# Late modulation with an output per partition: row sums on VectorE and one transposition per chunk

## What is computed

```python
def _modulation(cond, w_mod, b_mod):
    m = jax.nn.silu(cond) @ w_mod + b_mod          # cond [1024], w_mod [1024, 3072]
    return jnp.split(m, 3, axis=-1)
...
h = x * (1.0 + sc) + sh                            # before layer l's input projection
...
x_new = _layer_norm(DEEPNORM_ALPHA * x + (1.0 + g) * out, ln_g[l], ln_b[l])
```

## Time and profile before

| | us |
|---|---|
| median of 3 runs | 1850.63 (1850.36 to 1851.28) |
| the profiled execution, its own time | 1850.39 |
| its span in the profile | 1848.6 |
| PE busy | 1802.8 (98%) |
| DVE busy | 1291.5 (70%) |
| ACT busy | 928.0 (50%) |

### The profile page before, as it was taken

How to read it: one execution, slowest core, us unless ns; L and a number is a source line. 1 busy time by engine, 2 the same in 40 slices (tenths; PEclk the granted TensorE clock), 3 DMA queues, 4 the chain that set the end, 5 groups by cost and what they waited for, 6 DMA issues and landing times. The chain is left out here.

```text
span 1848.6 us, 30835 instructions
## 1 busy us (share of the span) xinstructions
PE 1802.8 (98%) x10621; PEld 1554.1 (84%) x10621; DVE 1291.5 (70%) x2061; ACT 928.0 (50%) x1680; POOL 269.4 (15%) x219
## 2 busy tenths in 40 slices
PE   7999999999999999989999999999999999999998
PEld 3888888888888888878878889888888888898886
DVE  6677777778687877765868485675848484757658
ACT  2555555555555555560046555464736464554500
POOL 3100000000000000255431010101000010102951
PEclk9999999999999999999999999999999999999999
DMA  9512121312122222225420010101010100101343
GB/s 348 135 47 83 47 82 47 84 38 79 54 74 60 74 60 62 73 94 187 159 80 24 12 45 11 45 0 45 11 45 11 34 23 11 45 11 45 99 143 125
DMA packets 82111, 127.28 MB, mean 69 GB/s; under 512 B 49760, under 2 KB 49920, under 8 KB 81936
## 3 DMA queue, kind: packets, MB, share of 16 engines
q1 hardware_dynamic: 76048, 108.54, 18.7%
q0 software_dynamic: 2384, 8.39, 1.6%
q10 hardware_dynamic: 3632, 9.73, 1.3%
HBM read 108.90 MB, written 20.09 MB: 70 GB/s over the span
## 5 line engine op out<-in xcount | busy, mean ns | idle before, releaser
L548 PE MATMUL acc<-h_hi,w_hi 128*128 128x512 f32 (+1 forms) x1408 | 524.9, 373 | 3.1 <-DVE h_lo L473 1.6
L548 PE MATMUL acc<-h_hi,w_lo 128*128 128x512 f32 (+1 forms) x1408 | 508.7, 361 | 0.0
L548 PE MATMUL acc<-h_lo,w_hi 128*128 128x512 f32 (+1 forms) x1408 | 507.9, 361 | 0.0
L548 PEld LDWEIGHTS acc<-h_hi,w_lo 128*128 128x128 f32 x1408 | 265.3, 188 | 41.5
L548 PEld LDWEIGHTS acc<-h_hi,w_hi 128*128 128x128 f32 x1408 | 265.8, 189 | 40.3 <-DVE h_lo L473 4.7
L548 PEld LDWEIGHTS acc<-h_lo,w_hi 128*128 128x128 f32 x1408 | 266.3, 189 | 33.9
L1676 DVE TENSOR_REDUCE stats<-acc 128x1 f32<-128x1280 f32 x128 | 189.7, 1487 | 43.3 <-PE acc L1775 42.7
L1586 ACT ACTIVATE far_prob<-acc,stats 128x1280 f32<-128x1280 f32 x128 | 170.2, 1330 | 28.3 <-DVE stats L1676 26.5
L1593 ACT ACTIVATE far_pt<-acc 128x512 f32<-128x512 f32 (+1 forms) x192 | 101.1, 527 | 162.0 <-PE acc L1784 158.6
L1775 PE MATMUL acc<-k_dup,q_stack 128*128 128x512 f32 (+1 forms) x768 | 176.7, 367 | 1.8 <-ACT far_prob L1586 0.4
L1797 PE MATMUL acc<-far_pt,far_v 128*128 128x128 f32 x1280 | 172.7, 275 | 0.0
(11 more groups left out here) (208 smaller groups left out, 2906.8 us busy)
## 6 DMA issues: line engine op xcount, KB each, us to landing
w_raw<-in_w_in SPq DMA_DIRECT2D x64, 512.0 KB, 3.3
near_late_slots<-in_w_mod SPq DMA_DIRECT2D x64, 256.0 KB, 2.7
w_raw<-in_w_out SPq DMA_DIRECT2D x16, 512.0 KB, 3.2
w_raw<-y_t POOLq DMA_DIRECT2D x14, 448.0 KB, 5.0
y_t<-y SPq DMA_DIRECT2D x7, 640.0 KB, 3.1
modulation_rows<-in_w_scale SPq DMA_DIRECT2D x8, 512.0 KB, 6.9
modulation_rows<-in_w_mod SPq DMA_DIRECT2D x8, 512.0 KB, 6.7
out_rows<-in_x SPq DMA_DIRECT2D x8, 512.0 KB, 4.5
```

What stands on the lines that cost most here:

```text
L548: mm = nc.tensor.matmul(m.bank(self.bank_of(j, c), w), wt[:, b % 2, k, :], ht[:, k, t0:t0 + w], start=(k == 0 and i == 0), stop=(k == KT - ...
```

## The change

The weights of the late modulation are given transposed (`w_late`, 4096 x 1024): a tile is now 128 outputs, one per partition, by 512 inputs. A chunk's 512 outputs are four blocks of 128 (t = 0 to 3), each in two halves of the inputs; tile u is half u // 4, block u % 4. `sum(u)` is a `tensor_tensor_reduce` per vector: the tile times the condition laid along the row, summed along it, 128 x 512, with the sum of the first half as the start value of the second. The result is a column. After eight tiles there are 8 columns (two vectors, four blocks), and PE turns them once (`turn`), [128, 8] to [8, 128].

For this the condition has to stand in each partition as a row. At the start PE turns it, ACT copies it and SP stores it to HBM (`cond_rows`). In the chunks `load_coef` spreads half of it (512 values of both vectors) over 128 partitions: a copy of 512 KB, twice a chunk, into one buffer. The copy of the second half waits until `sum(3)` is done, `sum(4)` waits until it has landed.

The sums move too. `dve_part` now has 0, 1, (2, 3), (4, 5), (6), where it had 0, 1, 2, 3, 4; only `sum(7)` is left for the steps (step 7, in the last chunk step 3). The tile 7 is loaded with 5 and 6. `reduce_last` is gone. The row is stored by two copies in place of one.

```diff
     def load(self, sp, c, u):
         if u >= 2:
-            sp.wait_ge(self.summed, CREDIT + c * 2 * KT + 2 * (u - 1))
+            sp.wait_ge(self.summed, CREDIT + c * 2 * KT + 2 * (KT if u == KT else u - 1))
...
+    def load_coef(self, sp, c, half):
+
+        sp.wait_ge(self.summed, CREDIT + c * 2 * KT + KT * half)
+        first = self.cond_rows[0, half % 2 * 512:half % 2 * 512 + 1]
+        src = bass.AP(first.tensor, first.offset, [[0, P], [D, 2], [1, 512]])
+        sp.dma_start(self.coef, src).then_inc(self.coef_loaded, 16)
 
     def sum(self, v, c, u):
+
+        half, t = u // 4, u % 4
         v.wait_ge(self.loaded[u % 2], CREDIT + c * 8 * KT + 16 * (u // 2 + 1))
+        if t == 0:
+            v.wait_ge(self.coef_loaded, CREDIT + c * 32 + 16 * (half + 1))
         if u == 0:
-            v.wait_ge(self.reduced, CREDIT + c * 1)
+            v.wait_ge(self.turned, CREDIT + c * 1)
+        v.wait_ge(self.summed, CREDIT + c * 2 * KT + 2 * u)
+        x = self.slots[u % 2]
         for cnd in range(2):
...
-                ins = self.nc.vector.scalar_tensor_tensor(self.acc[cnd], x, coef, self.acc[cnd], ALU.mult, ALU.add)
-            ins.then_inc(self.summed, 1)
...
+            self.nc.vector.tensor_tensor_reduce(out=unused, in0=x, in1=self.coef[:, cnd, :], scale=0.5,
+                                                scalar=self.sums[:, 0, col:col + 1] if half else 0.0, op0=ALU.mult, op1=ALU.add,
+                                                accum_out=self.sums[:, half, col:col + 1]).then_inc(self.summed, 1)
...
+    def turn(self, pe, c, bank):
 
         pe.wait_ge(self.summed, CREDIT + c * 2 * KT + 2 * KT)
...
+        self.nc.tensor.transpose(self.m.psum[0:8, bank, 0:P], self.sums[:, 1, :], self.m.ident[:, :]).then_inc(self.turned, 1)
...
@@ dve_part
-        for j in range(6, self.cum[2]):
+        for j, sums in zip(range(6, self.cum[2]), ((2, 3), (4, 5), (6,))):
             self.split_x_lo(v, c, j)
-            late.sum(v, c, j - 4)
+            for u in sums:
+                late.sum(v, c, u)
...
@@ sync, chunk
-                    for u in (3, 4, 5, 6):
+                    for u in (3, 4):
+                        late.load(sp, c, u)
+                    late.load_coef(sp, c, 1)
+                    for u in (5, 6, 7):
                         late.load(sp, c, u)
...
@@ sync, start
                 modulation.load_weights(sp)
+                modulation.store_cond(sp)
                 load_first(sp)
...
                 if g == 1:
+                    sp.wait_ge(modulation.cond_stored, 16)
                     p[0].load(sp, 0, 1)
...
@@ vector, steps
-                        if step == 3 and last:
-                            late.sum(v, c, 5)
-                        if NU - 3 <= step < NU and not last:
-                            late.sum(v, c, step - NU + 3 + 5)
+                        if step == (3 if last else NU - 3):
+                            late.sum(v, c, KT - 1)
...
@@ tensor, step 10
-                            if last:
-                                late.reduce_last(pe, c, 1)
-                            else:
-                                late.reduce(pe, c, 7)
+                            late.turn(pe, c, 1 if last else 7)
```

More of the change, by code:

```diff
@@ L237, in activate @@
         act.wait_ge(self.small_in, 48)
-        self.nc.scalar.activation(self.m.cond_act[:, :, :], self.m.cond[:, :, :], ACT.Tanh, scale=0.5).then_inc(self.tanh_done, 1)
+        self.nc.scalar.activation(self.m.cond_act[:, :, :], self.m.cond[:, :, :], ACT.Tanh, scale=0.5).then_inc(self.act, 1)
     def exp_lambda(self, act):
         act.wait_ge(self.dve, 2)
-        self.nc.scalar.activation(self.sums[:, 2:4], self.sums[:, 0:2], ACT.Exp).then_inc(self.lam_exp, 1)
+        self.nc.scalar.activation(self.sums[:, 2:4], self.sums[:, 0:2], ACT.Exp).then_inc(self.act, 1)
     def take_rows(self, act):
@@ L368, with __init__ @@
     AHEAD = 2
-    def __init__(self, nc, m, near, stack, w_mod, mod_rows):
-        self.nc, self.m, self.w_mod, self.mod_rows = nc, m, w_mod, mod_rows
+    def __init__(self, nc, m, near, stack, w_late, cond_rows, mod_rows):
+        self.nc, self.m, self.w_late, self.cond_rows, self.mod_rows = nc, m, w_late, cond_rows, mod_rows
         sem = lambda n: stack.enter_context(nc.semaphore("x_" + n))
         self.slots = [near.late_slots[:, i, :] for i in range(2)]
-        self.acc = [near.late_acc[:, i, :] for i in range(2)]
-        self.row = near.late_row
+        self.coef, self.row, self.sums = near.late_coef, near.late_row, near.late_sums
+        self.unused = [near.prob[:, 2 + i, 0:512] for i in range(2)]
@@ L400, in sum @@
-            ins.then_inc(self.summed, 1)
-    def reduce(self, pe, c, bank):
-        pe.wait_ge(self.summed, CREDIT + c * 2 * KT + 2 * KT)
[L405 to L417, removed]
-            mm = self.nc.tensor.matmul(self.m.psum[0:2, bank, :], self.m.pick[:, cnd, :], self.acc[cnd],
-                                       start=False, stop=(cnd == 1))
-        mm.then_inc(self.reduced, 1)
+            col = cnd * 4 + t
@@ L422, in take_row @@
     def take_row(self, act, c, bank):
-        act.wait_ge(self.row_stored, CREDIT + c * 16)
-        act.wait_ge(self.reduced, CREDIT + c * 1 + 1)
-        self.nc.scalar.activation(self.row, self.m.psum[0:2, bank, :], ACT.Copy, scale=0.5).then_inc(self.row_ready, 1)
+        act.wait_ge(self.row_stored, CREDIT + c * 32)
+        act.wait_ge(self.turned, CREDIT + c * 1 + 1)
+        self.nc.scalar.activation(self.row, self.m.psum[0:8, bank, 0:P], ACT.Copy).then_inc(self.row_ready, 1)
     def store_row(self, sp, c):
@@ L428, in store_row @@
         sp.wait_ge(self.row_ready, CREDIT + c * 1 + 1)
-        sp.dma_start(self.mod_rows[:, bass.ds(c * 512 + ROW_PAD, 512)], self.row).then_inc(self.row_stored, 16)
+        for cnd in range(2):
+            sp.dma_start(self.mod_rows[cnd, bass.ds(c * 4 + ROW_PAD // P, 4), :], self.row[4 * cnd:4 * cnd + 4, :]).then_inc(self.row_stored, 16)
 TOKEN_TILES = [range(0, 4), range(4, 8), range(8, 10)]
@@ L961, in of_result, with neighbourhood @@
         return t.rearrange("p (b r n) -> p b r n", b=2, r=2) if self.local else t.rearrange("p (b n) -> p b n", b=2)
-def neighbourhood(nc, m, near, stack, p, modulation, tokens, x_in, load_first, all_counters, out_w, after, biases, w_mod, mod_rows, y_out):
+def neighbourhood(nc, m, near, stack, p, modulation, tokens, x_in, load_first, all_counters, out_w, after, biases, w_late, cond_rows, mod_rows, y_out):
     l = 0
@@ L979, in neighbourhood @@
     factors_ready, spread, gate_scaled = sem("factors_ready"), sem("spread"), sem("gate_scaled")
-    late = LateModulation(nc, m, near, stack, w_mod, mod_rows)
+    late = LateModulation(nc, m, near, stack, w_late, cond_rows, mod_rows)
     counters += late.counters
@@ L1086, in chunk @@
                             out_w.load(sp, p, k)
-                            if k == 3:
-                                late.load(sp, c, 7)
                     else:
@@ L1098, in chunk @@
                     if not last:
-                        for u in (7, KT, KT + 1):
+                        for u in (KT, KT + 1):
                             late.load(sp, c, u)
+                        late.load_coef(sp, c, 2)
                     late.store_row(sp, c)
@@ L1119, in _ @@
                     late.load(sp, 0, u)
+                late.load_coef(sp, 0, 0)
                 each_chunk(sp, chunk)
-                sp.wait_ge(late.row_stored, CREDIT + 16 * NCH)
+                sp.wait_ge(late.row_stored, CREDIT + 32 * NCH)
                 sp.wait_ge(y_stored, CREDIT + 16 * (NCH - 1))
@@ L1156, in _ @@
                 modulation.activate(act)
+                modulation.take_cond(act)
                 p.split_hi_part(act, 0, 0)
```

75 lines of the change are left out of this document (40 added, 35 removed).

## The result

| | before | after |
|---|---|---|
| median of eight runs each (us) | 1850.32 (1850.07 to 1851.28) | 1855.53 (1854.56 to 1856.89) |
| the profiled execution | 1850.39, span 1848.6 | 1855.38, span 1853.5 |

The account below looks back on a forecast made before the run. PE was taken as the bound, busy 1802.8 of 1848.6 us. Seven loop chunks -1.9, last chunk -1.96 and start +0.2 gave -3.65 us, so 1847.0 against the median; range 1845 to 1855.

Parts of the forecast that it names:

- How large is L?: `dve_part`: L, the time from `load_coef`'s issue to landing, ahead of `sum(4)`; taken as 3.4 us, bounds 3.3 and 5.7.
- rival 2: Condition lands very late, by repeated reads of the same HBM rows or a later tile 6: 1858 at L = 5.7; chance 0.15.
- The threshold: Scores of unit 1, loop chunks: PE stalls once the copy's landing time L passes 4.1 us, by L - 4.1 a chunk.
- rival 1: Condition lands a little late, L of 4.4 to 4.7: 2.1 to 4.2 us of stall, 1849 to 1851; chance 0.23.
- The last chunk: Chunk's end: without `reduce_last` the values product L1398 starts 1.96 us earlier, at the low part's end, and all is kept.
- No stall up to L = 5.2: Last chunk, `dve_part`: no weight split there gives 1.15 us more slack, so PE does not stall up to that landing time.
- second deadline: `dve_part`: last `split_x_lo`, needed by the scores of unit 0, comes at 281.0 + L against 285.7; decides from L = 4.7.
- `reduce` as cover: Chunk's end: `reduce` covers PE's wait for the low part, so removing it gains 0.27 us a loop chunk, 1.96 in the last.
- Rival 3: All of `reduce` is won, PE not waiting for the low part: 1.68 us x 7 and 3.4, -15, 1836; chance 0.05.
- Length of a sum: DVE: `tensor_tensor_reduce` of 512 columns takes 714 ns, 1.4 us for a tile; sums cost as before but for 0.5 at `sum(0)`.
- Moving the sums: DVE, steps 7 to 9: 2.8 us of sums leave steps 8 and 9, where PE never waits for DVE; worth nothing.
- The start: Before the first chunk: one more transposition, the condition's store and its first copy cost +0.2 us (0 to 2.5).

Follow-up runs that it names:

- e7: Changed kernel, the condition copied as one 4 KB piece of one row per partition, in place of two of 2 KB; 1851.55 us, ratio 1.0004.
- e2: Changed kernel, the condition's copy reading 128 different rows of `w_late` (4 KB pieces) in place of the same rows for all partitions; 1848.25 us, ratio 0.9987.
- e3: Changed kernel, every condition copy but the first taking half of the values (256 KB, 1 KB pieces); 1848.76 us, ratio 0.9993.
- e1: Changed kernel with `sum(4)` moved to just ahead of `gate_silu` and sums 5 and 6 to step 0; 1847.05 us, ratio 0.9981.
- e4: Kernel before, `reduce` of the loop chunks on 64 columns in place of 512, other outputs left out; 1848.32 us, ratio 0.9988.
- e9: Kernel before, with only its sums 5 and 6 moved into `dve_part` of the loop chunks, as the change has them; 1851.36 us, ratio 1.0003.
- e6: e1 with two k-steps of the next chunk's projection moved behind the transposition at the chunk's end; 1838.04 us, ratio 0.9933 to the kernel before.
- e8: Changed kernel, the condition's second half loaded long before into its own buffer, sums left in place; 1847.32 us, ratio 0.9983.

## Why the prediction was wrong

**Which step failed.** "How large is L?": 3.4 was taken, with bounds of 3.3 and 5.7, nearer to the weights' row than to the gate row's; it measured 4.3 to 5.4 in the loop chunks. The choice went by what lay beside the gate row's copy in time. It discounted the gate row's 4.4 because a copy of POOL was beside it. e7 has the gate row's form (pieces of 4 KB from one row) with nothing but its own tile beside it, and lands after 4.5: so the 4.4 needed no discount. What the two spread copies had in common, that all partitions read one row, was named in rival 2 as a cause and set aside with the argument that no other copy is in flight. That argument was wrong: rows of their own save 0.8 us at the same bytes and pieces (e2 against e7). And the copy is not of the gate row's form: it has two pieces of 2 KB for each partition where the gate row has one of 4, which was left out of the sum and costs 0.6 (5.1 against 4.5). The Trainium skill's rule ("DMA: Bandwidth & Descriptors", section "Anatomy of one DMA"; 2.0 us plus bytes over 436 GB/s, by which 3.2 us is the estimate for 512 KB) holds in this trace for the weights (3.3) and not for the spread copy (5.0). The price of the step: 7 x 0.94 = 6.6 us of the 8.5.

**The threshold was right.** Stalls from 4.1 us on, by L - 4.1: the table by chunk above shows it within 0.1 us, and e7 once more with other landings. `gate_silu` was to start at 283.9 + L; with the chunk 1.62 us later and this chunk's landing of 4.75 that gives 290.27, and it started at 290.43. So rival 1 and rival 2 were the same mechanism as the forecast with another L; the outcome lies between them.

**The last chunk** was a second miss, 1.5 us. "No stall up to L = 5.2" moved only the deadline at the scores of unit 1; the prediction's own second deadline, the last split before the scores of unit 0 (281.0 + L against 285.7), has no weight split ahead of it and stays at 4.7. The landing of 4.29 in this chunk keeps it, with the sums at their usual length. The meeting of `sum(4)` with a GpSimd instruction made one of them 1.85 us longer, and 281.0 + 4.29 + 1.85 - 285.7 = 1.4 us is what PE waits there (1.35). That the late landing itself brought it there is not so (e2 and e3 land sooner and have it too); e1 has a meeting of 1.67 us as well, but with the last split ahead of the sums, and gains the full 1.99. The cause is read from the two instructions' ends and the four kernels; a kernel with the GpSimd instruction elsewhere was not tried.

**`reduce` as cover: right.** Forecast 0.27 a chunk and 1.96 in the last; e1 shows 0.27 and 1.99, e4 shows 0.31, and L1407 waits 1.30 us for the low part, as said. Rival 3 is refuted by e4.

**Length of a sum: near.** 0.71 was taken for 512 columns; 0.69 was measured, and 0.75 for those with a start value, with 0.61 and 0.68 from one start to the next.

**Moving the sums: free**, as the prediction had it for steps 7 to 9 (e9: +0.03%, within the interval). **The start**: forecast +0.2, measured +0.29.

**After this stage** 0.4 us are left (1006.3 from the first `out_rows<-mod_rows` to the end, against 1005.9), where the change moves nothing. That is scatter: the eleven profiles have 1005.6 to 1006.4 there. With it the sum closes: against the forecast 6.6 (loop) + 1.5 (last chunk) + 0.1 (start) + 0.4 = 8.6 of 8.5 us.

## What to carry to other kernels

Work taken from the engine that sets the pace is worth only what it covers nothing with: here 0.3 of 1.7 us a time, and the rest came only when other work was put in the hole (e6). A new copy in front of an engine that runs in order must be priced by the nearest copy with the same way of reading and the same pieces, not by one of the same size; where its landing is in doubt by more than the slack, either load it earlier (e8) or put what depends on it behind what others wait for (e1). If the slack is known to a tenth (4.1 us here) and the landing only between 3.3 and 5.7, the chances should follow the landing.

## What was unexpected of the hardware

One row of HBM spread over 128 partitions, 512 KB in pieces of 2 KB, lands in 4.3 to 5.4 us in these chunks; in pieces of 4 KB, still of one row, in 4.1 to 4.9; with a row of its own for each partition, in pieces of 4 KB too, in 3.5 to 4.1; 256 KB of one row, in pieces of 1 KB, in 3.8 to 4.2. Half of the bytes thus saves about 1 us, though the row is read as often.

A VectorE instruction of 0.75 us with its operands in SBUF took 2.60 beside a GpSimd `tensor_tensor` of 2.63 us. Which instruction of the chain is hit changes with when the chain gets there: the second of `sum(4)` after the change, the first in e7 (2.63), one behind the last split in e1 (1.67).
